# A gather of routed tokens as fp32 products by token tile, and one TensorE loop over expert pairs 1 to 14

## The reference, cut to what matters

```
h      = rms_norm(x) * norm_ffn_g                 # 256 x 1024
logits = h @ router_w + router_b                  # 32 experts
gates  = softmax(top 4 logits)
for each expert e, over the tokens that chose it:
    gate, up = split(h_e @ w_gate_up[e] + b_gate_up[e])     # 1024 -> 2 x 1024
    act      = (clip(up) + 1) * min(gate, 7) * sigmoid(1.702 * min(gate, 7))
    y       += gates[e] * (act @ w_down[e] + b_down[e])
```

## Time and profile before

| | us |
|---|---|
| median of 3 runs | 1185.32 (1185.07 to 1187.43) |
| profiled execution, its own time | 1184.91 |
| span from first to last instruction | 1183.2 |
| PE busy | 1104.2 (93%) |
| DVE busy | 350.3 (30%) |
| ACT busy | 167.0 (14%) |
| mean DMA rate over the span | 368 GB/s |

### The profile page before, as it was taken

One profiled execution on the slowest core, in us unless ns is written; L12 is line 12 of the kernel. 1 busy time (PEld: TensorE's weight loads), 2 busy tenths in 40 slices (PEclk: granted clock), 3 DMA queues, 4 the chain that ended last, 5 costly groups with the idle time before them and its releaser, 6 DMA issues.

```text
span 1183.2 us, 13909 instructions
## 1 busy us (share of the span) xinstructions
PE 1104.2 (93%) x5819; PEld 533.5 (45%) x5819; DVE 350.3 (30%) x741; ACT 167.0 (14%) x272; POOL 4.0 (0%) x23
## 2 busy tenths in 40 slices
PE   7999999999999999999898989898989898989897
PEld 5889886764334333433333333333334333333332
DVE  4685244454213212212121212122212212121213
ACT  3431233441101000000000010101010101010002
POOL 1000000000000000000000000000000000000000
PEclk9999999999999999999999999999989999999999
DMA  9832324667999999999999999999999999999996
GB/s 341 301 128 86 128 86 116 245 279 314 430 426 429 427 427 436 425 431 429 431 427 432 430 433 429 432 429 432 429 430 433 428 433 429 432 427 433 424 426 245
DMA packets 39605, 435.65 MB, mean 368 GB/s; under 512 B 5877, under 2 KB 5962, under 8 KB 20394
## 3 DMA queue, kind: packets, MB, share of 16 engines
q1 hardware_dynamic: 37642, 433.67, 87.3%
q10 hardware_dynamic: 1920, 1.34, 0.6%
HBM read 433.95 MB, written 1.05 MB: 368 GB/s over the span
## 4 chain that ended last, share of the span: by engine, by line
PE 62%; DMA 35%; DVE 1%; ACT 1%; issue 1%; SPq 0%; DVEq 0%; PEldq 0%
DMA ring<-in_w_down 34%; PE ps L2016 17%; PE ps L2061 17%; PE ps L1577 4%; PE ps L1688 4%; PE ps L2076 3%; PE ps L1634 3%; PE ps L1684 2%; PE ps L1557 2%; PE ps L1745 2%; PE ps L1985 2%; PE ps L1821 1%; PE ps L1865 1%; DMA ring<-in_w_in 1%; PE ps L2004 1%
## 5 line engine op out<-in xcount | busy, mean ns | idle before, releaser
L2061 PE MATMUL ps<-ring,work 128*64 128x512 f32 x1024 | 244.2, 626 | 40.9 <-DMA ring<-in_w_down 38.2
L2016 PE MATMUL ps<-ring,work 128*64 128x512 f32 x1024 | 225.6, 593 | 8.5 <-DMA ring<-in_w_gate_up 8.5
L2016 PE MATMUL ps<-work 128*64 128x512 f32 x1024 | 230.5, 592 | 0.0
L2061 PEld LDWEIGHTS ps<-ring,work 128*64 128x64 f32 x1024 | 80.1, 143 | 180.2 <-issue 162.9
L2016 PEld LDWEIGHTS ps<-ring,work 128*64 128x64 f32 x1024 | 71.4, 137 | 158.3 <-issue 141.2
L2016 PEld LDWEIGHTS ps<-work 128*64 128x64 f32 x1024 | 71.7, 137 | 136.3 <-issue 129.1
L1429 DVE TENSOR_SCALAR work<-ps 128x512 f32<-128x512 f32 x32 | 21.9, 686 | 197.1 <-PE ps L1557 197.1
L1452 DVE COPY work<-ps 128x512 f32<-128x512 f32 x16 | 11.1, 691 | 223.4 <-PE ps L1557 223.4
L1464 DVE COPY work<-ps 128x512 f32<-128x512 f32 (+1 forms) x16 | 11.1, 691 | 221.5 <-PE ps L2061 221.5
L2076 PE MATMUL ps<-work 128*128 128x512 f32 (+1 forms) x132 | 59.7, 608 | 10.4 <-ACT work L800 10.1
L1557 PEld LDWEIGHTS ps<-small,work 128*128 128x128 f32 (+1 forms) x354 | 44.9, 170 | 51.2 <-issue 45.1
(11 more groups left out here) (241 smaller groups left out, 728.3 us busy)
## 6 DMA issues: line engine op xcount, KB each, us to landing
work<-in_w_gate_up SPq DMA_DIRECT2D x64, 2048.0 KB, 36.6
ring<-in_w_gate_up SPq DMA_DIRECT2D x22, 4096.0 KB, 32.2
ring<-in_w_down SPq DMA_DIRECT2D x22, 4096.0 KB, 36.1
ring<-in_w_gate_up SPq DMA_DIRECT2D x20, 2048.0 KB, 21.6
ring<-in_w_down SPq DMA_DIRECT2D x17, 2048.0 KB, 20.4
ring<-in_w_in SPq DMA_DIRECT2D x7, 2048.0 KB, 15.5
ring<-in_xattn_w_kv SPq DMA_DIRECT2D x2, 2048.0 KB, 14.4
ring<-in_w_out SPq DMA_DIRECT2D x2, 2048.0 KB, 8.2
```

The lines of the kernel that those rows point to most:

```text
L2016: last = nc.tensor.matmul(bank(b)[p], xg_T[k][:, kb, :], quad_columns(w[:, kk, D_MODEL * (q // 2):D_MODEL * (q // 2 + 1)], q % 2), start=F ...
L2061: last = nc.tensor.matmul(bank(Y_BANK + y)[p], act_T[k][:, b, HALF * c:HALF * c + HALF], w[:, b, 512 * q:512 * q + 512], start=False, stop ...
```

## The change

Three edits.

1. The three bf16 parts are gone; ACT writes the scaled rows once as fp32 (`scaled_rows`), `pick` is fp32, and every gather is 2 tiles x 8 blocks = 16 fp32 products.
2. The opening gather is taken tile by tile: tile 0's slots are counted and picked before tile 1's experts are known, and `gather_first(0)` runs before the count of tile 1, `gather_first(1)` after it. `keep_turning` is gone.
3. TensorE's loop has five turns over pairs 1 to 14; in the last turn an `If` skips the third pair. Pairs 0 and 15 are written out. SP's loads are untouched.

```diff
-        split = [as_bf16(at, TILES * D_MODEL)... for at in (M2, M2 + 1024, QKT)]
-        remainder = [area(HT + 1024, D_MODEL), area(HT, D_MODEL)]
+        scaled_rows = area(M2, TILES, D_MODEL)
+        square_parts = area(HT + 1024, D_MODEL)
...
-        picks = as_bf16(HT + 1920, TILES * 2 * SLOTS)...
+        picks = area(QKT, TILES, 2 * SLOTS)
...
# ScalarE: split_high and split_mid become
+            def scale_rows(t):
                 act.wait_ge(S("x2_inverse"), t + 1)
                 for h in range(2):
+                    nc.scalar.activation(scaled_rows[:, t, half_cols(h)], half_of(t, h), ACT.Copy,
+                                         scale=by_tile(rstd, t)).then_inc(S("rows_scaled"), 1)
...
# VectorE: split_rest and split_low are gone; after x2_inverse(1):
+            v.wait_ge(S("first_slots_filled"), 1)
+            place_slots(0)
+            pick_tile(0, 0, 0).then_inc(S("first_tile_picked"), 1)
             choose_experts(1)
-            split_rest(1, 0)
-
             filled(v, "slots")
+            place_slots(1)
...
                 if first_one:
-                    pick_one(0, 0).then_inc(S("picked_first"), 1)
-                    split_rest(1, 1)
-                    split_low(1, 0)
-                    split_low(1, 1)
+                    pick_tile(0, 0, 1).then_inc(S("picked_first"), 1)
                     pick_one(1, 0).then_inc(S("picked"), 1)
...
# TensorE
             f_turn(1, 6, KB, 0)
+            pe.wait_ge(S("before_ready"), 2)
+            pe.wait_ge(S("chosen_ready"), 1)
+            take(pe, "slots")
+            mm(pair("slots")[:, 0:E], before, chosen_b[:, 0, :]).then_inc(S("first_slots_filled"), 1)
             router_logits(1, 4, 6, 3)
             router_logits(1, 6, KB, 0)
-            keep_turning(12)
+            pe.wait_ge(S("first_tile_picked"), 1)
+            gather_first(0)
             pe.wait_ge(S("chosen_ready"), TILES)
...
-            keep_turning(18)
...
+            def gather_first(t):
+                for b, columns in enumerate(block_columns):
+                    if b in (0, 2):
+                        pe.wait_ge(S("rows_scaled"), TILES * t + 1 + b // 2)
+                    last = nc.tensor.matmul(bank(GATHER_BANK[0])[:, SLOTS * b:SLOTS * b + SLOTS],
+                                            scaled_rows[:, t, columns], pick[0][:, t, :],
+                                            start=(t == 0 and b == 0), stop=(t == TILES - 1 and b == KB - 1))
+                return last
...
+            def gather_both():
+                for b, columns in enumerate(block_columns):
+                    for t in range(TILES):
+                        last = nc.tensor.matmul(bank(GATHER_BANK[b // 4])[:, P * (b % 4):P * (b % 4) + P],
+                                                scaled_rows[:, t, columns], picks[:, t, :],
+                                                start=(t == 0), stop=(t == TILES - 1))
...
-                for i in range(BY_HALVES):
-                    pair_of_experts(0, i, i, ...)
-                with pe.Fori(0, TURNS) as rev:
...
+                pair_of_experts(0, 0, 0, 1, 2, lambda c: first_pass_chunk(0, c), (0, 0, 0),
+                                opening=lambda: second_gather(0))
+                whole_turns = (PAIRS - 1) // TURN_PAIRS
+                with pe.Fori(0, whole_turns) as rev:
...
+                    one_of_turn(1)
+                    one_of_turn(2)
+                    with pe.If(rev < whole_turns - 1):
+                        one_of_turn(3)
+                i = PAIRS - 1
+                pair_of_experts(0, i, i, ..., final=True, pieces=True)
```

More of the change, by code:

```diff
@@ L1376, in pick_one @@
                 for t in range(TILES):
[L1377 to L1378 removed]
+                    ins = pick_tile(k, i, t)
                 return ins
@@ L1942, in _ @@
-            pe.wait_ge(S("before_ready"), 2)
+            block_columns = [slice(j, 256, 2) for j in range(2)] + [slice(256 + j, 768, 4) for j in range(4)] \
+                + [slice(768 + j, 1024, 2) for j in range(2)]
+            def gather_first(t):
[6 more added lines that the diff above has]
+                return last
@@ new lines, in gather @@
+            def gather(k):
+                for b, columns in enumerate(block_columns):
+                    for t in range(TILES):
+                        last = nc.tensor.matmul(bank(GATHER_BANK[k])[:, SLOTS * b:SLOTS * b + SLOTS],
+                                                scaled_rows[:, t, columns], pick[k][:, t, :],
+                                                start=(t == 0), stop=(t == TILES - 1))
+                last.then_inc(S("gather_filled"), 1)
+            def gather_both():
+                for b, columns in enumerate(block_columns):
+                    for t in range(TILES):
+                        last = nc.tensor.matmul(bank(GATHER_BANK[b // 4])[:, P * (b % 4):P * (b % 4) + P],
+                                                scaled_rows[:, t, columns], picks[:, t, :],
+                                                start=(t == 0), stop=(t == TILES - 1))
+                    if b % 4 == 3:
+                        last.then_inc(S("gather_filled"), 1)
@@ L1952, in _ @@
             last.then_inc(S("count_filled"), 1)
-            drained(pe, "f_T1")
             pe.wait_ge(S("logits_moved"), TILES)
-            keep_turning(18)
[L1958 to L1987, removed]
-                        last.then_inc(S("gather_filled"), 1)
@@ L1990, in _, with kind_of_place @@
             low, high = slice(0, HALF), slice(HALF, P)
+            def kind_of_place(s):
+                return 1 if s >= RING else 2 if s in [second for _, second in TWIN_PLACES] else 0
             def chunk_landed(s, loads, turned16):
                 if loads is not None:
-                    pe.wait_ge(S(f"slot_loaded{s}"), turned16[s >= RING] + 16 * (loads + 1))
+                    pe.wait_ge(S(f"slot_loaded{s}"), turned16[kind_of_place(s)] + 16 * (loads + 1))
                 return place(s)
@@ L2131, in begin_pass @@
                 pe.wait_ge(S("picked_first"), PAIRS * r + 1)
-                gather(0, opening)
+                if opening:
+                    gather_first(1).then_inc(S("gather_filled"), 1)
+                else:
+                    gather(0)
             def second_gather(r):
```

68 lines of the change are left out of this document (20 added, 48 removed).

## The result

The changed kernel takes **1223.37 us** (median of 4 runs, 1221.84 to 1225.51) against 1185.32 before: ratio 1.0321, 95% interval 1.0306 to 1.0336. The forecast was 1186.7, range 1183.5 to 1191.0. A fourth run of the kernel before, at 1919.98 us, is slow by itself and is not counted. The profiled execution took 1225.51 us, its span is 1223.7.

What follows compares the result with a forecast made beforehand. The weight stream's start and rate, level with PE at the end, were taken to bound the kernel; +1.3 (opening) + 1.16 (last gather) - 1.1 (fetches) = +1.4 us on 1185.3 gave 1186.7, range 1183.5 to 1191.0.

Steps and rivals of the forecast that it cites:

- three signs of being wrong: Gather records at 0.107 us or less or 0.13 or more, fetches not falling by about half, a gap before pair 15.
- I cost it at nothing: TensorE's loop branches, including the new If, were priced at 0 us, as queued gather work covers them.
- the three pairs of a turn stay in place: TensorE's loop: the code of three pairs is held between rounds, read from no fetches in 660:1010 of the earlier trace.
- Rival (c): Slower by a stall: 2 us uncovered at the exit before pair 15, +3.4, or a clock fall, +3.1; chance 0.10.
- I take 0.12 us a record: Each fp32 gather record on TensorE costs 0.12 us, with bounds 0.107 and 0.19.
- Rival (b): Slower by strided fp32 weight loads: each 0.01 us a record more costs 0.96; +4.3 at 0.15, +8 at 0.19; chance 0.24.
- the loop's saving of 1.1: TensorE's loop: about 9 fewer code fetches inside the stream at 0.12 us each, -1.1 us (0 to -1.4).
- I expect none here: Opening without idle transposes: no clock fall expected despite gaps of 0.9 and 0.5 us; up to 1.7 us if it falls.
- the drawn opening: Predicted opening: gate_up begins at 270.75, gather(1) takes 3.84 us, and the second weight request comes at 281.9.
- The gather's tail of +1.16: The gather before pair 15, where PE sets the pace: 3.84 us for 2.68, +1.16 us (+0.7 to +3.4).
- +1.3: Opening: the second weight request comes at 281.9 instead of 280.55, so the stream runs 1.3 us later.
- The pair of 54 us: From pair 1 on, PE's period is about 54 us against the stream's 58.5, so the dearer gather is hidden.

Runs made afterwards that it cites:

- e6: The changed kernel with its loop turn moved by 100 instructions of empty waits at the start of TensorE's program; 1200.05 us, ratio 1.0118.
- e10: The changed kernel with its loop turn moved by only 50 instructions of empty waits, placed in an idle wait of TensorE; 1195.39 us, ratio 1.0086.
- e2: The kernel before with the new loop alone, bf16 gathers and idle transposes kept; 1190.96 us, ratio 1.0046.
- e1: The changed kernel with the old loop, fp32 gather and opening by tiles kept; 1198.76 us, ratio 1.0110.
- e5: e1 with the scaled rows packed so that each stationary block of the gathers is contiguous; 1190.69 us, ratio 1.0045.
- e8: e5 with eight idle transposes into an unused bank behind the slot products; 1187.78 us, ratio 1.0020.
- e11: The kernel before with the new loop alone, its turn moved by 152 filler instructions in three idle waits; 1190.00 us, ratio 1.0042.
- e13: e8 with the second gather moved between gate_up chunks 2 and 3, old loop and no fillers; 1185.10 us, ratio 1.0003.
- e12: e13 with the new loop in place of the old, its turn moved by 50 filler instructions in an idle wait; 1182.85 us, ratio 0.9986.

## Why the prediction was wrong

All three signs of being wrong that the prediction named came: gather records of 0.18 us, 45 fetches in the stream where 10 or 11 were expected, and a gap of 3.73 us before pair 15.

**The step that failed first: the branches, "I cost it at nothing", resting on "the three pairs of a turn stay in place".** It was read from the earlier trace rows that TensorE holds a turn of three pairs, and taken as a property of three pairs. It depends on where they lie (e6, e10). The changed program starts its turn seven blocks earlier and, as it happens, near the end of a block; by the count above it touches eight blocks, and the turn is fetched again in every round (9 fetches from one return to the next; e10 has one at 502.1 us and the next at 1154.5). The gap at the first return is 4.05 + 1.96 us, and half clock follows, which costs another 3.4 us (6.8 us at half speed). The whole price is larger by about 1 us that neither row shows: by the starts of the gathers, the pair with a return in it takes 66.3, 66.3, 65.9 and 66.1 us, and the same pair in e10 takes 55.9. That is 10.0 to 10.4 a turn. A turn of three pairs takes 167.7 us in e10 (501.33 to 668.99) and 178.0 as changed (499.35 to 677.38). The stream needs 3 x 58.5 = 175.5. So the stall alone (e2: 3 x 52.9 and 9.3 more, 168) or the dear gather alone (e1) stays under the stream's pace, and together they pass it.

The sum closes: four returns are 40.9 us, and from the last gather to the end it is 68.8 us for 63.4 in e10, another 5.4; together 46.3. In e10 PE waits for the stream again from its ninth pair on, which costs it 14.3 us. That leaves 32.0. The opening of e10 is 2.0 us later, so 30.0 remain, and the profiled executions differ by just that (spans of 1223.7 and 1193.7 us; the medians by 28.0).

Rival (c) had this stall, but only before pair 15, as "2 us uncovered". It priced the branch, and not the refetch of everything behind it.

The Trainium skill, "Runtime: NRT & Kernel Launch", section "Instruction fetch mechanics", says that a taken branch out of the window of fetched pages waits for a fetch. The trace agrees, with 3.5 to 4.4 us at a return. The section gives that window as two pages, but it also gives TensorE an instruction memory of 2048 instructions, which is eight of its blocks of 256. The two pages do not fit here, since turns that touch seven blocks came back without a fetch (e10). The eight blocks do: e10 fetches one block at its first return (502.1 us) and then none, as if seven were held and one fetched ahead. That this is the reason is not shown.

**"I take 0.12 us a record."** For stride 2 it is 0.118, for stride 4 0.233, and with half the blocks of either kind 0.18 (86.6 / 480) is the mean. The upper bound of 0.19 held; the value was taken from four transposes of stride 4 that cost 0.02 more than contiguous ones. Those were the nearest rows, but none of the kernel before shows a gather product with an fp32 stationary block of that stride. Why its load doubles between stride 2 and 4, and a transpose's doesn't, no run tells. e5 shows the size: 0.117 when contiguous. Rival (b) had the mechanism: at 0.18 it gives +1.4 + 0.96 x 6 = +7.2, or +8.3 without the loop's saving of 1.1; e1 is +13.1, some 5.0 of it the clock in the opening (below), which leaves 8.1.

**The clock: "I expect none here".** It fell for 10.2 us and once more for 3.4. Set against the drawn opening, the second request came 7.2 us late (289.09 for 281.9): the opening began 1.7 earlier, strided loads took 1.1 + 1.1 + 2.0 more, and half clock took about 0.8 (gather_first(1)) + 0.3 + 2.3 (chunk 0) + 1.6 (chunk 1) more. The row for a clock that stays full came from another stretch, with products of 128 and 512 columns, and did not carry over to gather products of 64 columns with a gap of 0.75 us between them. With contiguous loads the fall is 6.8 us long (e5), and eight transposes in the gap keep the clock full (e8); the second request is 3.1 us earlier for it.

**What held.** The stream and its start bound the end: from e5 to e8 the request is 3.1 us earlier and the ratio 0.25% lower, 3.0 us, though the two intervals overlap. The gather's tail of +1.16 is about +1.0 when contiguous (3.73 for 2.68 to 2.84). With its own premises granted, the sum is right: e8, contiguous loads and full clock and the old loop, was to be +1.3 + 1.16 = +2.5 us; it is 1.0020, +2.4 (by its interval -0.7 to +5.3), with the second request at 281.88 for 281.9. The code that isn't fetched, -1.1, is -1.5 in e11 and -2.25 from e13 to e12. The pair of 54 us is 53.9 in e12 (320.2 to 374.1 between the same gaps), 56.0 as changed. So three premises failed (the held turn, the price of a record, the clock) and not the arithmetic.

**What stays open.** That moving the turn decides is shown (e6, e10). Whether the offset of 0.07 to 0.19 block is what it seems is not; and that the limit is seven blocks is inferred from the places of the kernels here, all with turns of 6.2 to 6.6 blocks. It also stays open why e2 shows no gap at its exit and the changed kernel does, and how ten fetches come to be worth 1.5 to 2.3 us, where the GB/s of the two stretches of the earlier trace rows gave 0.16 each.

## What to carry to other kernels

A loop that runs without fetching its code is only known to do so at its present place: before code ahead of a long loop is shortened or lengthened, or the loop is moved, count in which 16 KB blocks it starts and ends, and read the instruction queue's fetch count after, before anything else. Slack is spent once: two costs, each hidden alone, have to be added against the same slack. A price for a weight load is taken from a weight load of the same type and the same stride, and where none is in the trace, the upper bound has to be taken as likely too.

## What the hardware showed that was not expected

- Whether TensorE keeps a loop's code across the return depends on where the code lies: shifted by 0.2 block of 256 instructions, the same turn went from 9 fetches a round to none, and 28.0 us went (after, e10). The places fit a limit of seven blocks touched. Where the turn is fetched anew, PE stands still for 3.5 to 4.4 us and then 0.8 to 2.0 (5.9 to 6.3 in one piece with the bf16 gather, e2).
- In the gathers an fp32 weight load of 128 columns takes 0.117 us contiguous (e5), 0.118 at a stride of 2 words, 0.233 at a stride of 4 (after, 499.4 to 504.9 us, clock 1.00).
- An empty instruction with two waits that are already met costs TensorE up to 0.10 us (e11: 75 in 7.84 us): fillers are no free way to move code.
- In the opening's chain of 64-column fp32 products with a gap of 0.75 us the granted clock was 0.50 for 10.2 us (6.8 with contiguous loads, e5); with eight transposes in the gap as well it stayed at 1.00 (e8).
